# The residual row travels with each expert's rows instead of being read back at the end

## The chip, the cores and the metric

One core of a Trainium2 chip runs the whole program. The metric is the device time of one execution in microseconds; lower is better.

## What is computed

One layer of a hybrid decoder trunk on 512 tokens of width 1024, fp32 throughout: a token-mixing block (attention, convolution, matrix memory), then a hierarchical mixture of experts, then a gated per-layer embedding and a last RMSNorm. The parts that matter here, with `x2` for the residual after token mixing:

```
h2  = rmsnorm(x2) * g_ffn
wts = p_group * softmax(top-2 logits)            # each token goes to 2 of 32 experts
x3  = x2 + sum over its 2 experts of wts * (silu(h2 @ w_gate[e]) * (h2 @ w_up[e])) @ w_down[e]
hp  = rmsnorm(x3) * g_ple
x4  = x3 + sigmoid(hp @ w_ple_gate) * (p @ w_ple_proj)
out = rmsnorm(x4) * g_final
```

## The kernel before

The program is written by hand, engine by engine: the order in which instructions stand in each engine's block is the order in which they run, and semaphores are the only link between engines.

**Experts.** `x2` is stored to `x2_rows` in memory. The 32 experts run one after the other, each on a block of up to 64 tokens. A token's row of 1024 is handled as two halves of 512, so a block fills 128 partitions. For expert n:

- GpSimd (`gather_rows`) gathers the block's rows of `x2` by an indirect DMA into `xr[n % 4]` (`ROWS` = 4 slots).
- TensorE (`turn_block`, L1518) transposes them into one PSUM bank. VectorE (`turned_block`, L2200) scales them into `xT`.
- TensorE (`up`) multiplies by the gate and up weights. ScalarE takes the sigmoid (L1004), VectorE makes the product (`swiglu`, L2207 and L2209), TensorE transposes it (L1538) and ScalarE copies it (L1009).
- TensorE (`down`) multiplies by the down weights. ScalarE (`scale_rows`, L1016) multiplies the result by the routing weight into `yr[n % 4]`, and raises `y_scaled`.
- GpSimd (`scatter_rows`) scatters `yr` into `expert_rows` in memory, which has one row per token for each of its two choices.

TensorE's order in iteration n is `up(n)` (with the transpose of the hidden block of n-1 in its middle), `turn_block(n+1)`, `down(n-1)`. The weights (3 MB per expert) come over SyncE's queue into a ring of 7 slots for gate and up and 9 for down; a load is issued when TensorE has released its slot. Experts with more than 64 tokens would take further blocks in a conditional loop behind; with these inputs that loop runs no block.

**Tail.** After the last `down`, TensorE multiplies `p` by its projection (`ple`, into PA and PB; ScalarE and VectorE copy the halves, L1043 and L2236). `w_ple_gate` is split into a rounded part (`round_pg`, ScalarE, L1024) and a remainder (`pg_remainder`, VectorE, L2230), eight pieces each. When every scatter has landed, SyncE reads back the rows of both choices (`yk[t]`, L671 and L674) and `x2` (`x2_row_back`, L642), in four tiles of 128 tokens. VectorE adds them (L2262, L2263), TensorE transposes the sum (L1405), ScalarE rounds it (`h3_rounding`, L1063), VectorE takes the remainder (L2254), and TensorE runs the eight gate products, each as high x high, low x high and high x low (L1108, `pg_mm`). The factor of the RMSNorm enters as the scale of the sigmoid.

Of the kernel before, what the change touches and what calls it, by code (L numbers as in the profile page):

```python
# [31 lines left out]
ALU = mybir.AluOpType  # L32
ACT = mybir.ActivationFunctionType
AXX = mybir.AxisListType.X

P = 128
D = 1024
SEQ = 512
T = SEQ // P
KD = D // P  # L40
# [10 lines left out]
NEXP = NGROUP * PER_GROUP  # L51
HID = 256
PLE = 256
EPS = 1e-6
# [69 lines left out]
def build(nc, x, consts, chan, g_mix, r_bias, g_final, w_cm, w_tm, w_if, w_gate, w_branch, w_out,  # L124
# [5 lines left out]
    with ExitStack() as ctx:  # L130
# [378 lines left out]
        def _(sp):  # L509
# [130 lines left out]

            def x2_row_back(t):
                sp.dma_start(x_sb[:, t, :], x2_rows[t * P:(t + 1) * P, :]).then_inc(rows_loaded[t], 16)  # L642

            sp.wait_ge(up_done, 28)
# [4 lines left out]
            sp.dma_start(pg_w[1], w_pg[1, :, :]).then_inc(pg_loaded[1], 16)  # L649
            for t in range(2):  # L650
                x2_row_back(t)
            sp.wait_ge(routed, 1)
# [12 lines left out]
            for t in range(T):  # L665
                if t >= 2:
                    x2_row_back(t)
                if t == 0:
                    for cols, loaded in ((slice(0, 512), rows_loaded[0]), (slice(512, D), gmix_then_rows_loaded)):
                        for k in range(2):  # L670
                            sp.dma_start(yk[0][:, k, cols], expert_rows[k * SEQ:k * SEQ + P, cols]).then_inc(loaded, 16)  # L671
                    continue
                for k in range(2):
                    sp.dma_start(yk[t][:, k, :],  # L674
                                 expert_rows[k * SEQ + t * P:k * SEQ + (t + 1) * P, :]).then_inc(rows_loaded[t], 16)
                if t == 1:
                    sp.dma_start(gfin_sb, g_final.partition_broadcast(P)).then_inc(params_loaded, 16)
# [11 lines left out]
        def _(act):  # L689
            roots = [0]  # L690

            def root(dst, total, squared, count):

                roots[0] += 1
                act.wait_ge(squared, count)
                act.activation(dst, total, ACT.Sqrt, scale=1.0 / D, bias=chn[:, EPS_COL:EPS_COL + 1]).then_inc(rooted, 1)

# [312 lines left out]

            def scale_rows(n, b2, slot, scattered):

                act.wait_ge(down_done, n + 1)
                if scattered is not None:
                    act.wait_ge(rows_scattered[slot], scattered)
                act.activation(yr[slot], Y[b2][:, :], ACT.Copy, scale=table_w(0, n)).then_inc(y_scaled, 1)  # L1016

            act.wait_ge(table_ready, 2)
# [8 lines left out]
            for n in range(NEXP + 1):  # L1027
                if n:
                    hidden_copy(n - 1, (n - 1) % 2)
                if n < NEXP:  # L1030
                    gate_sigmoid(n, n % 2)
                if n:
                    m = n - 1
                    scale_rows(m, m % 2, m % ROWS, m // ROWS * 16 if m >= ROWS else None)
                if n == OVER_KNOWN:
                    act.wait_ge(routed, 1)
                    n_over = act.value_load(ctl[0:1, 0:1], min_val=0, max_val=MAX_OVER)
# [13 lines left out]
            with act.If(n_over > 0):  # L1051
                with act.Fori(0, MAX_OVER) as j:
                    with act.If(j < n_over):
                        gate_sigmoid(NEXP + j, 0)
                        hidden_copy(NEXP + j, 0)
                        scale_rows(NEXP + j, 0, 0, SCATTERED + j * 16)

# [8 lines left out]
            for t in range(T):  # L1066
# [5 lines left out]
                act.activation(junk3, x_sb[:, t, :], ACT.Square, accum_out=ss3[:, t:t + 1]).then_inc(x3_squared, 1)  # L1072
            root(rr3, ss3, x3_squared, T)
            act.wait_ge(tail_rstd, 1)
# [572 lines left out]
        def _(dve):  # L1647
# [25 lines left out]

            def rstd(root, total, done=None, offset=EPS):

                rooted_seen[0] += 1
                dve.wait_ge(rooted, rooted_seen[0])
                steps[0] += 1
                dve.tensor_scalar(total, total, 1.0 / D, offset, ALU.mult, ALU.add).then_inc(dve_step, 1)
                chain(dve.reciprocal(root, root))  # L1680
                if root.shape[-1] == 1:
                    chain(dve.scalar_tensor_tensor(total, total, root, root, ALU.mult, ALU.mult))
                else:
                    chain(dve.tensor_tensor(total, total, root, ALU.mult))
                    chain(dve.tensor_tensor(total, total, root, ALU.mult))
                chain(dve.tensor_scalar(total, total, -0.5, 1.5, ALU.mult, ALU.add))
                last = dve.tensor_tensor(root, root, total, ALU.mult)
                if done:
                    last.then_inc(done[0], 1)
                    dve.wait_ge(*done)  # L1690
                else:
                    chain(last)
# [451 lines left out]
            dve.wait_ge(act_step, 7)  # L2144
            chain(dve.tensor_scalar(per[:, 5, 0, :], per[:, 0, 0, :], 1.0, None, ALU.add))
            chain(dve.reciprocal(per[:, 5, 0, :], per[:, 5, 0, :]))
# [58 lines left out]
            def swiglu(n, b2):  # L2205
# [3 lines left out]
                dve.tensor_tensor(hs[b2], GU[b2][:, P:2 * P], sgx[b2], ALU.mult).then_inc(h_swished, 1)  # L2209

            turned_block(0, 0)
            for n in range(NEXP):
                if n + 1 < NEXP:
                    turned_block(n + 1, (n + 1) % 2)
                swiglu(n, n % 2)
                if n == 0:
                    over_slots()
                if n == 1:
                    over_experts()
                if n == 3:  # L2220
                    over_rows()
                if n == OVER_KNOWN:
                    dve.wait_ge(routed, 1)
                    n_over = dve.value_load(ctl[0:1, 0:1], min_val=0, max_val=MAX_OVER)

            def pg_remainder(k):
# [11 lines left out]
            for t in range(3):  # L2238
                ple_second_half(t)
                pg_remainder(2 * t)  # L2240
                pg_remainder(2 * t + 1)
            with dve.If(n_over > 0):
                with dve.Fori(0, MAX_OVER) as j:
                    with dve.If(j < n_over):
                        turned_block(NEXP + j, 0)
                        swiglu(NEXP + j, 0)


# [8 lines left out]
            for t in range(T):  # L2257
                dve.wait_ge(rows_loaded[t], 48)
                for cols in (slice(0, D),) if t else (slice(0, 512), slice(512, D)):
                    if cols.start:  # L2260
                        dve.wait_ge(gmix_then_rows_loaded, 48)
                    chain(dve.tensor_tensor(x_sb[:, t, cols], x_sb[:, t, cols], yk[t][:, 0, cols], ALU.add))  # L2262
                    dve.tensor_tensor(x_sb[:, t, cols], x_sb[:, t, cols], yk[t][:, 1, cols], ALU.add).then_inc(x3_ready, 1)  # L2263
                if t == 0:
                    ple_second_half(3)
                    h3_remainder(0)
                    for k in range(6, KD):
                        pg_remainder(k)
                if t == 1:
                    h3_remainder(1)  # L2270
            rstd(rr3, ss3, (tail_rstd, 1))
            for t in range(T - 1):
                if t == T - 2:
                    h3_remainder(T - 1)
                for half in range(2):
# [4 lines left out]
                    chain(dve.tensor_tensor(ple_rows[t][:, cols], ple_rows[t][:, cols], sg6[:, t % 2, cols], ALU.mult))  # L2280
                dve.tensor_tensor(x_sb[:, t, :], x_sb[:, t, :], ple_rows[t], ALU.add).then_inc(x4_ready, 1)
                if t == 0:
# [7 lines left out]
            for piece, cols in enumerate(LAST_COLUMNS):  # L2290
                dve.wait_ge(pg_sig, 2 * T - 1 + piece)  # L2291
                chain(dve.tensor_tensor(ple_rows[t][:, cols], ple_rows[t][:, cols], sg6[:, 1, cols], ALU.mult))  # L2292
                chain(dve.tensor_tensor(x_sb[:, t, cols], x_sb[:, t, cols], ple_rows[t][:, cols], ALU.add))  # L2293
                dve.tensor_tensor_reduce(out=sg6[:, 0, cols], in0=x_sb[:, t, cols], in1=x_sb[:, t, cols], scale=1.0 / D,  # L2294
# [16 lines left out]
        def _(pool):  # L2311
# [52 lines left out]
            for n in range(NEXP):  # L2364
                slot = n % ROWS
                if n + ROWS < NEXP:
                    pool.wait_ge(rows_turned, n + 1)
                    gather_rows(slot, table[:, 0, n + ROWS:n + ROWS + 1], rows_gathered[slot])
                pool.wait_ge(y_scaled, n + 1)
                scatter_rows(slot, table[:, 1, n:n + 1], rows_scattered[slot])  # L2370
                if n == OVER_KNOWN:
                    pool.wait_ge(routed, 1)
                    n_over = pool.value_load(ctl[0:1, 0:1], min_val=0, max_val=MAX_OVER)
# [93 lines left out]
```

## Time and profile before

| | us |
|---|---|
| median of 3 runs | 933.08 (932.34 to 934.02) |
| the profiled execution | 934.07 |
| its span, first to last instruction | 931.9 |
| mean granted TensorE clock | 0.992 |
| PE busy | 898.1 (96%) |
| DVE busy | 504.0 (54%) |
| ACT busy | 343.2 (37%) |
| POOL busy | 195.8 (21%) |

PE is TensorE, DVE VectorE, ACT ScalarE, POOL GpSimd, SPq SyncE's queue. A busy share over the whole span says little here, since the stages have different limits. The experts run from about 638 to 855 us, the tail from there to the end.

### The profile page before, as it was taken

Reading aid. Unit: us, or ns where it says so; the run is one execution under the profiler, and the core shown is the slowest. Engines: PE = TensorE matmul, PEld = TensorE weight load, DVE = VectorE, ACT = ScalarE, POOL = GpSimd, SP = SyncE. Lnnn points to the kernel's source line nnn. Section 1 sums busy time; section 2 is a strip of 40 time slices with the busy share of each in tenths; the row PEclk is TensorE's granted clock in tenths of the full one; section 3 lists DMA queues with packets and bytes.
Section 4 is the critical chain, followed back from the end, with each engine's and each line's share of the span. In section 5 each row is a group of like instructions: output and inputs, shape, how many; then the busy total and the mean of one; then the engine's idle time right before and its main releaser. Section 6 shows DMA issues by size and latency. Waiting matters only on the chain. (4 is left out here: it accounts for less than half of the span.)

```text
span 931.9 us, 12362 instructions
## 1 busy us (share of the span) xinstructions
PE 898.1 (96%) x4864; PEld 661.8 (71%) x4864; DVE 504.0 (54%) x1043; ACT 343.2 (37%) x571; POOL 195.8 (21%) x169
## 2 busy tenths in 40 slices
PE   6999999999999999999999999999999999888896
PEld 5788788878877887888888888876555555444586
DVE  6378579759767999943333336375112112111766
ACT  5534453535355357622222243121122122112465
POOL 0052263327134433000000000002332332311000
PEclk9999999999999999999999999999999999999899
DMA  7520321122031111541222209959999999999701
GB/s 280 181 91 23 126 78 46 71 88 65 27 114 45 44 60 46 212 167 71 92 102 102 101 9 396 383 198 412 420 417 420 422 416 422 418 421 392 272 23 68
DMA packets 29233, 180.35 MB, mean 194 GB/s; under 512 B 5856, under 2 KB 6368, under 8 KB 18040
## 3 DMA queue, kind: packets, MB, share of 16 engines
q1 hardware_dynamic: 24056, 171.16, 46.8%
q0 software_dynamic: 5120, 8.41, 2.4%
q8 instruction: 39, 0.64, 0.3%
q14 instruction: 18, 0.15, 0.0%
HBM read 175.33 MB, written 12.59 MB: 202 GB/s over the span
## 5 line engine op out<-in xcount | busy, mean ns | idle before, releaser
L1108 PE MATMUL bank<-mT_parts,low_parts 128*128 128x512 f32 (+1 forms) x456 | 178.6, 394 | 0.0
L1108 PE MATMUL bank<-arena,cst 128*64 128x256 f32 (+2 forms) x918 | 133.5, 431 | 7.6 <-DMA arena<-in_w_expert 6.9
L1108 PE MATMUL bank<-mT_parts,x_parts 128*128 128x512 f32 (+1 forms) x328 | 132.7, 405 | 2.8 <-DVE arena L1783 2.3
L1108 PE MATMUL bank<-hT_parts,x_parts 128*128 128x512 f32 (+1 forms) x328 | 129.1, 394 | 0.0
L1718 DVE TENSOR_TENSOR low_parts<-arena,x_parts 128x1024 fp32r<-128x1024 f32 (+1 forms) x44 | 64.6, 1470 | 93.7 <-ACT x_parts L718 93.3
L2200 DVE TENSOR_TENSOR cst<-bank,chn 128x512 f32<-128x512 f32 x32 | 22.1, 692 | 164.8 <-PE bank L1518 164.8
L1108 PEld LDWEIGHTS bank<-arena,cst 128*64 128x64 f32 (+1 forms) x918 | 63.5, 138 | 61.6 <-issue 28.6
L1108 PEld LDWEIGHTS bank<-mT_parts,low_parts 128*128 128x128 f32 (+1 forms) x456 | 84.9, 186 | 21.5 <-DVE low_parts L1718 0.4
L1770 DVE SCALAR_TENSOR_TENSOR arena<-arena,chn 128x512 f32<-128x512 f32 x116 | 99.1, 912 | 0.0
L2351 POOL DMA_INDIRECT mT<-x_rows,table x32 | 33.1, 1034 | 270.5 <-DVE table L2130 257.8
L1108 PE MATMUL bank<-arena 128*128 128x64 f32 (+9 forms) x400 | 79.8, 332 | 0.0
L1108 PEld LDWEIGHTS bank<-mT_parts,x_parts 128*128 128x128 f32 (+1 forms) x328 | 61.0, 186 | 19.6 <-DVE low_parts L1718 3.5
L2336 POOL TENSOR_TENSOR arena<-arena 128x128 f32<-128x128 f32 (+3 forms) x32 | 38.6, 1208 | 172.6 <-ACT arena L814 172.6
L1108 PEld LDWEIGHTS bank<-hT_parts,x_parts 128*128 128x128 f32 (+1 forms) x328 | 61.0, 186 | 15.3 <-issue 1.0
L1108 PEld LDWEIGHTS bank<-arena 128*128 128x128 f32 (+1 forms) x400 | 56.4, 189 | 19.6 <-issue 13.6
L2357 POOL DMA_INDIRECT expert_rows<-mT,table x32 | 32.5, 1016 | 148.9 <-ACT mT L1016 144.3
L814 ACT ACTIVATE arena<-arena,small 128x384 f32<-128x384 f32 (+3 forms) x32 | 32.6, 1020 | 57.0 <-DVE small L1870 56.9
L959 ACT ACTIVATE arena<-bank 128x512 f32<-128x512 f32 x24 | 14.2, 597 | 102.3 <-PE bank L1108 95.2
L1108 PE MATMUL bank<-mT_parts,cm_high_b 128*128 128x512 f32 x128 | 51.2, 409 | 0.3 <-ACT mT_parts L724 0.3
L1108 PE MATMUL bank<-hT_parts,cm_high_b 128*128 128x512 f32 x128 | 49.2, 393 | 0.0
L1016 ACT ACTIVATE mT<-bank,table_weight 128x512 f32<-128x512 f32 x32 | 22.0, 687 | 67.0 <-PE bank L1108 67.0
L1108 PE MATMUL bank<-x_parts,mT_parts 128*128 128x384 f32 x128 | 44.7, 350 | 0.0
(303 smaller groups left out, 1592.7 us busy)
## 6 DMA issues: line engine op xcount, KB each, us to landing
arena<-in_w_expert SPq DMA_DIRECT2D x19, 2048.0 KB, 28.8
arena<-in_w_expert SPq DMA_DIRECT2D x30, 1024.0 KB, 19.9
arena<-in_w_cm SPq DMA_DIRECT2D x32, 512.0 KB, 3.5
arena<-in_w_gate SPq DMA_DIRECT2D x7, 1536.0 KB, 6.7
hT<-in_w_expert SPq DMA_DIRECT2D x4, 2048.0 KB, 24.5
yT<-in_w_expert SPq DMA_DIRECT2D x4, 2048.0 KB, 27.5
arena<-in_w_tm SPq DMA_DIRECT2D x4, 1536.0 KB, 7.1
arena<-in_w_branch SPq DMA_DIRECT2D x8, 768.0 KB, 8.0
```

The costliest lines, as they stand in the source:

```text
L814: act.activation(sc[:, u % 2, 0:n], sc[:, u % 2, 0:n], ACT.Exp, bias=nmx[:, u % 2:u % 2 + 1], accum_out=den[:, u:u + 1]).then_inc(exps_don ...
L959: act.activation(sgm[:, br], (PA, PB, S_16)[br][:, :], ACT.Sigmoid).then_inc(gate_read, 1)
L1016: act.activation(yr[slot], Y[b2][:, :], ACT.Copy, scale=table_w(0, n)).then_inc(y_scaled, 1)
L1108: return pe.matmul(out, lhsT, rhs, start=start, stop=stop)
L1718: dve.tensor_tensor(low, weights, high.bitcast(F32), ALU.subtract).then_inc(done, 1)
L1770: dve.scalar_tensor_tensor(cacc[:, j % 2], ypad[:, j:j + SEQ], weight, cacc[:, j % 2], ALU.mult, ALU.add).then_inc(conv_step, 1)
L2200: dve.tensor_tensor(xT[b2], TR[:, :].rearrange("p (k h s) -> p k h s", k=KD // 2, h=2), chn[:, G_FFN:G_FFN + KD].rearrange("p (h k) -> p k ...
L2336: pool.tensor_tensor(dst[:, 0:n], sc[:, u % 2, 0:n], sc[:, u % 2, n:2 * n], ALU.add).then_inc(pool_step, 1)
L2351: pool.indirect_dma_start(out=xr[slot], out_offset=None, in_=x2_halves, in_offset=bass.IndirectOffsetOnAxis(ap=token_halves, axis=0), boun ...
L2357: pool.indirect_dma_start(out=expert_halves, out_offset=bass.IndirectOffsetOnAxis(ap=row_halves, axis=0), in_=yr[slot], in_offset=None, bo ...
```

## The change

Each expert's result now carries the residual row with it: `weighted_rows` computes `yr = weight * Y + xr` on VectorE, where `xr` is the row gathered for this block. Every token goes to two experts, so the sum of its two rows holds `x2` twice; the routing weights are doubled to match, `x_sb` then holds `2 * x3`, and the tail halves it (the factors in the two RMSNorm roots, 0.5 in the sums that form `x4`). `x2` is no longer read back, and of two additions per tile of the tail one is left. The first two pieces of the diff are SyncE's, the third is ScalarE's, the last is GpSimd's, the others are VectorE's.

```
-            for t in range(2):
-                x2_row_back(t)
...
-                if t >= 2:
-                    x2_row_back(t)
...
-                if n:
-                    m = n - 1
-                    scale_rows(m, m % 2, m % ROWS, m // ROWS * 16 if m >= ROWS else None)
...
-            chain(dve.tensor_scalar(per[:, 5, 0, :], per[:, 0, 0, :], 1.0, None, ALU.add))
+            chain(dve.tensor_scalar(per[:, 5, 0, :], per[:, 0, 0, :], 1.0, 0.5, ALU.add, ALU.mult))
...
+            def weighted_rows(n, b2, slot, scattered):
+                dve.wait_ge(down_done, n + 1)
+                if scattered is not None:
+                    dve.wait_ge(rows_scattered[slot], scattered)
+                dve.scalar_tensor_tensor(yr[slot], Y[b2][:, :], table_w(0, n), xr[slot],
+                                         ALU.mult, ALU.add).then_inc(y_scaled, 1)
...
                 swiglu(n, n % 2)
+                if n:
+                    weighted_rows(n - 1, (n - 1) % 2, (n - 1) % ROWS, (n - 1) // ROWS * 16 if n > ROWS else None)
...
-                    chain(dve.tensor_tensor(x_sb[:, t, cols], x_sb[:, t, cols], yk[t][:, 0, cols], ALU.add))
-                    dve.tensor_tensor(x_sb[:, t, cols], x_sb[:, t, cols], yk[t][:, 1, cols], ALU.add).then_inc(x3_ready, 1)
+                    dve.tensor_tensor(x_sb[:, t, cols], yk[t][:, 0, cols], yk[t][:, 1, cols], ALU.add).then_inc(x3_ready, 1)
...
             for n in range(NEXP):
                 slot = n % ROWS
-                if n + ROWS < NEXP:
-                    pool.wait_ge(rows_turned, n + 1)
-                    gather_rows(slot, table[:, 0, n + ROWS:n + ROWS + 1], rows_gathered[slot])
                 pool.wait_ge(y_scaled, n + 1)
                 scatter_rows(slot, table[:, 1, n:n + 1], rows_scattered[slot])
+                if n + ROWS < NEXP:
+                    gather_rows(slot, table[:, 0, n + ROWS:n + ROWS + 1], rows_gathered[slot])
```

On GpSimd, at the start of the experts, the gathers (mT<-x_rows) and scatters (expert_rows<-mT) stand like this before; `xr` and `yr` both lie in mT:

```order
L2351 DMA mT<-x_rows,table 128x512 [waits x2_spilled,table_ready]
L2351 DMA mT<-x_rows,table 128x512 x3
L2351 DMA mT<-x_rows,table 128x512 [waits rows_turned]
L2357 DMA expert_rows<-mT,table 2048x512 [waits y_scaled]
L2351 DMA mT<-x_rows,table 128x512 [waits rows_turned]
L2357 DMA expert_rows<-mT,table 2048x512 [waits y_scaled]
```

and like this in the changed kernel:

```order
L2348 DMA mT<-x_rows,table 128x512 [waits x2_spilled,table_ready]
L2348 DMA mT<-x_rows,table 128x512 x3
L2354 DMA expert_rows<-mT,table 2048x512 [waits y_scaled]
L2348 DMA mT<-x_rows,table 128x512
L2354 DMA expert_rows<-mT,table 2048x512 [waits y_scaled]
```

Five gathers stood ahead of scatter 0 and four do now. The gather for expert n+4 stood right behind scatter n-1 and needed only the transpose of expert n; it now stands behind scatter n, and so behind `y_scaled` of expert n.

On VectorE, between the last expert and the products of the tail, before:

```order
L2230 SCALAR_TENSOR_TENSOR pg_low_57<-arena,chn,pg_high_59 128x1024 [waits rounded] x2
...
L2262 TENSOR_TENSOR x_sb<-x_sb,arena 128x512 [waits rows_loaded0]
L2263 TENSOR_TENSOR x_sb<-x_sb,arena 128x512 [waits dve_step]
L2262 TENSOR_TENSOR x_sb<-x_sb,arena 128x512 [waits gmix_then_rows_loaded]
L2263 TENSOR_TENSOR x_sb<-x_sb,arena 128x512 [waits dve_step]
L2236 COPY arena<-bank 128x512 [waits ple_mm]
L2254 TENSOR_TENSOR hT_parts<-bank,mT_parts 128x4x128 [waits h_rounded] x2
L2230 SCALAR_TENSOR_TENSOR pg_low_57<-arena,chn,pg_high_59 128x1024 [waits rounded] x2
```

and in the changed kernel:

```order
L2259 TENSOR_TENSOR x_sb<-arena 128x512 [waits rows_loaded0]
L2259 TENSOR_TENSOR x_sb<-arena 128x512 [waits gmix_then_rows_loaded]
L2225 SCALAR_TENSOR_TENSOR pg_low_57<-arena,chn,pg_high_59 128x1024 [waits rounded]
L2231 COPY arena<-bank 128x512 [waits ple_mm]
L2251 TENSOR_TENSOR hT_parts<-bank,mT_parts 128x4x128 [waits h_rounded] x2
L2225 SCALAR_TENSOR_TENSOR pg_low_57<-arena,chn,pg_high_59 128x1024 [waits rounded] x3
```

Two remainder pieces stood ahead of the first addition and now stand behind it; the first tile takes two additions where it took four.

## Rows read from the trace of the kernel before

**Rows 1.** Page, part 2: DMA in 40 slices, mean busy share in tenths

```profile
DMA  7520321122031111541222209959999999999701
```

**Rows 2.** TensorE's timeline: start us, us, engine, line, what, count, wait and releaser

```profile
668.01 0.66 PE L1518 MATMUL bank<-cst,mT 128*128 128x128 f32 x4
...
775.43 0.66 PE L1518 MATMUL bank<-cst,mT 128*128 128x128 f32 x4
...
777.79 1.90 PE L1108 MATMUL bank<-yT,cst 128*64 128x256 f32 x16
```

**Rows 3.** Timeline of all engines, 699 to 713 us

```profile
702.17 0.69 ACT L1016 ACTIVATE mT<-bank,table_weight 128x512 f32<-128x512 f32 x1 [2.09 <-PE bank L1108]
703.66 1.02 POOL L2357 DMA_INDIRECT expert_rows<-mT,table  x1 [3.97 <-ACT mT L1016]
...
704.99 1.03 POOL L2351 DMA_INDIRECT mT<-x_rows,table  x1 [0.30 <-issue]
...
712.24 0.66 PE L1518 MATMUL bank<-cst,mT 128*128 128x128 f32 x4
```

**Rows 4.** The gathers (L2351) from 664 to 860 us: landing time

```profile
L2351 POOL DMA_INDIRECT mT<-x_rows,table x25: 1025/1029/1044, 667.1 to 823.0; - x25
...
DMA to landing us min/median/max: 7.9/9.2/10.7
```

**Rows 5.** The gathers from 638 to 664 us: landing time of three

```profile
DMA to landing us min/median/max: 6.9/7.6/9.2
```

**Rows 6.** GpSimd's timeline: the gather behind scatter 1

```profile
659.82 1.03 POOL L2351 DMA_INDIRECT mT<-x_rows,table  x1 [0.30 <-issue]
```

**Rows 7.** TensorE's timeline, late experts and the first products of the tail

```profile
822.22 3.63 PE L1108 MATMUL bank<-arena,cst 128*64 128x256 f32 x16 [2.12 <-DMA arena<-in_w_expert]
...
846.22 1.95 PE L1108 MATMUL bank<-arena,cst 128*64 128x256 f32 x16 [1.38 <-DMA arena<-in_w_expert]
...
855.31 7.13 PE L1108 MATMUL bank<-hT 128*128 128x512 f32 x16 [0.35 <-DMA hT<-in_pT]
863.24 7.13 PE L1108 MATMUL bank<-hT 128*128 128x512 f32 x16 [0.80 <-ACT yT L1043]
```

**Rows 8.** DMA issues, 630 to 860 us: KB each, median us to landing

```profile
arena<-in_w_expert SPq DMA_DIRECT2D x16, 2048.0 KB, 32.0
```

**Rows 9.** VectorE's scalar_tensor_tensor of 128x512: ns min/median/max

```profile
L1770 DVE SCALAR_TENSOR_TENSOR arena<-arena,chn x116: 735/747/1787, 68.2 to 344.9; 128x512 f32<-128x512 f32 x116
```

**Rows 10.** Timeline of the start of the tail

```profile
860.52 2.19 ACT L1024 ACTIVATE pg_high<-arena,chn 128x1024 fp32r<-128x1024 f32 x2 [2.51 <-DMA arena<-in_w_pg]
...
864.16 1.75 SPq L671 DMA_DIRECT2D arena<-expert_rows  x4
864.19 0.10 POOL L2391 MEMSET small<- 128x1 f32 x1 [6.74 <-DMA expert_rows<-mT,table]
...
869.19 2.17 ACT L1024 ACTIVATE pg_high<-arena,chn 128x1024 fp32r<-128x1024 f32 x2
...
870.08 0.68 DVE L2262 TENSOR_TENSOR x_sb<-x_sb,arena 128x512 f32<-128x512 f32 x1
...
873.57 0.60 ACT L1063 ACTIVATE mT_parts<-bank 128x512 fp32r<-128x512 f32 x1 [0.67 <-PE bank L1405]
...
874.22 3.78 PE L1108 MATMUL bank<-pg_high,mT_parts 128*128 128x512 f32 x8 [0.69 <-ACT mT_parts L1063]
874.81 2.47 DVE L2230 SCALAR_TENSOR_TENSOR pg_low<-arena,chn,pg_high 128x1024 fp32r<-128x1024 f32 x2
...
880.79 2.03 PE L1108 MATMUL bank<-pg_low,mT_parts 128*128 128x512 f32 x8
```

**Rows 11.** Windows: busy us of PE, PEld, DVE, ACT, POOL, PEclk, DMA share, GB/s

```profile
664.00:804.00 140.00, 139.23 (x992) 71.41 (x988) 25.96 (x66) 29.99 (x67) 45.05 (x44) 1.00 1.01 420
```

**Rows 12.** Windows of 1 us in the tail, the same columns

```profile
863.00:864.00 1.00, 0.76 (x2) 0.49 (x3) 1.00 (x1) 1.00 (x2) 0.00 (x0) 1.00 0.28 115
...
875.00:876.00 1.00, 1.00 (x4) 0.81 (x3) 1.00 (x2) 0.20 (x2) 0.00 (x0) 0.50 1.04 426
```

More of the change, by code:

```diff
@@ L639, in _ @@
             down_weights(NEXP - 1)
-            def x2_row_back(t):
-                sp.dma_start(x_sb[:, t, :], x2_rows[t * P:(t + 1) * P, :]).then_inc(rows_loaded[t], 16)
             sp.wait_ge(up_done, 28)
@@ L690, in _, with root @@
             roots = [0]
-            def root(dst, total, squared, count):
+            def root(dst, total, squared, count, scale=1.0 / D):
                 roots[0] += 1
                 act.wait_ge(squared, count)
-                act.activation(dst, total, ACT.Sqrt, scale=1.0 / D, bias=chn[:, EPS_COL:EPS_COL + 1]).then_inc(rooted, 1)
+                act.activation(dst, total, ACT.Sqrt, scale=scale, bias=chn[:, EPS_COL:EPS_COL + 1]).then_inc(rooted, 1)
             act.wait_ge(cell_set, 1)
@@ L1009, in hidden_copy @@
                 act.activation(hx[b2], HT[:, 0:P].rearrange("p (j s) -> p j s", j=2), ACT.Copy).then_inc(hx_ready, 1)
[L1011 to L1016, printed above, removed]
             act.wait_ge(table_ready, 2)
@@ L1055, in _ @@
                         hidden_copy(NEXP + j, 0)
-                        scale_rows(NEXP + j, 0, 0, SCATTERED + j * 16)
             def h3_rounding(t):
@@ L1072, in _ @@
                 act.activation(junk3, x_sb[:, t, :], ACT.Square, accum_out=ss3[:, t:t + 1]).then_inc(x3_squared, 1)
-            root(rr3, ss3, x3_squared, T)
+            root(rr3, ss3, x3_squared, T, 0.25 / D)
             act.wait_ge(tail_rstd, 1)
@@ L1672, in _, with rstd @@
             rooted_seen = [0]
-            def rstd(root, total, done=None, offset=EPS):
+            def rstd(root, total, done=None, offset=EPS, factor=1.0):
                 rooted_seen[0] += 1
@@ L1678, in rstd @@
                 steps[0] += 1
-                dve.tensor_scalar(total, total, 1.0 / D, offset, ALU.mult, ALU.add).then_inc(dve_step, 1)
+                dve.tensor_scalar(total, total, factor * factor / D, offset, ALU.mult, ALU.add).then_inc(dve_step, 1)
                 chain(dve.reciprocal(root, root))
@@ L1686, in rstd @@
                 chain(dve.tensor_scalar(total, total, -0.5, 1.5, ALU.mult, ALU.add))
-                last = dve.tensor_tensor(root, root, total, ALU.mult)
+                last = (dve.tensor_tensor(root, root, total, ALU.mult) if factor == 1.0 else
+                        dve.scalar_tensor_tensor(root, root, factor, total, ALU.mult, ALU.mult))
                 if done:
@@ L2224, in _ @@
                     n_over = dve.value_load(ctl[0:1, 0:1], min_val=0, max_val=MAX_OVER)
+            weighted_rows(NEXP - 1, (NEXP - 1) % 2, (NEXP - 1) % ROWS, (NEXP - 1) // ROWS * 16)
             def pg_remainder(k):
@@ L2239, in _ @@
                 ple_second_half(t)
-                pg_remainder(2 * t)
-                pg_remainder(2 * t + 1)
+                if t < 2:
+                    pg_remainder(2 * t)
+                    pg_remainder(2 * t + 1)
             with dve.If(n_over > 0):
@@ L2246, in _ @@
                         swiglu(NEXP + j, 0)
+                        weighted_rows(NEXP + j, 0, 0, SCATTERED + j * 16)
             def h3_remainder(t):
@@ L2257, in _ @@
             for t in range(T):
-                dve.wait_ge(rows_loaded[t], 48)
+                dve.wait_ge(rows_loaded[t], 32)
                 for cols in (slice(0, D),) if t else (slice(0, 512), slice(512, D)):
@@ L2261, in _ @@
                         dve.wait_ge(gmix_then_rows_loaded, 48)
-                    chain(dve.tensor_tensor(x_sb[:, t, cols], x_sb[:, t, cols], yk[t][:, 0, cols], ALU.add))
-                    dve.tensor_tensor(x_sb[:, t, cols], x_sb[:, t, cols], yk[t][:, 1, cols], ALU.add).then_inc(x3_ready, 1)
+                    dve.tensor_tensor(x_sb[:, t, cols], yk[t][:, 0, cols], yk[t][:, 1, cols], ALU.add).then_inc(x3_ready, 1)
                 if t == 0:
+                    pg_remainder(4)
                     ple_second_half(3)
                     h3_remainder(0)
-                    for k in range(6, KD):
+                    for k in range(5, KD):
                         pg_remainder(k)
@@ L2270, in _ @@
                     h3_remainder(1)
-            rstd(rr3, ss3, (tail_rstd, 1))
+            rstd(rr3, ss3, (tail_rstd, 1), factor=0.5)
             for t in range(T - 1):
@@ L2280, in _ @@
                     chain(dve.tensor_tensor(ple_rows[t][:, cols], ple_rows[t][:, cols], sg6[:, t % 2, cols], ALU.mult))
-                dve.tensor_tensor(x_sb[:, t, :], x_sb[:, t, :], ple_rows[t], ALU.add).then_inc(x4_ready, 1)
+                dve.scalar_tensor_tensor(x_sb[:, t, :], x_sb[:, t, :], 0.5, ple_rows[t], ALU.mult, ALU.add).then_inc(x4_ready, 1)
                 if t == 0:
@@ L2292, in _ @@
                 chain(dve.tensor_tensor(ple_rows[t][:, cols], ple_rows[t][:, cols], sg6[:, 1, cols], ALU.mult))
-                chain(dve.tensor_tensor(x_sb[:, t, cols], x_sb[:, t, cols], ple_rows[t][:, cols], ALU.add))
+                chain(dve.scalar_tensor_tensor(x_sb[:, t, cols], x_sb[:, t, cols], 0.5, ple_rows[t][:, cols], ALU.mult, ALU.add))
                 dve.tensor_tensor_reduce(out=sg6[:, 0, cols], in0=x_sb[:, t, cols], in1=x_sb[:, t, cols], scale=1.0 / D,
```

## The prediction

> **What bounds the kernel now.** I read first the busy shares in 40 slices, and there the DMA row [rows 1]: it stands at 9 from about 640 to 855 us, the stage of the experts, so this stage seems to end when the weights have come. Then TensorE's own timeline in it [rows 2]: the transposes of expert 5 stand at 668.01 and those of expert 22 at 775.43, so TensorE takes 107.42 / 17 = 6.32 us per expert, and in the windows it is busy for 139.23 of the 140 us up to 804, at full clock [rows 11]. So up to there TensorE bounds and the weights are ahead; the ring hides that they come more slowly. Then it turns, and TensorE waits for weights again and again [rows 7]; the gate and up products of expert 31 start at 846.22 behind such a wait. At TensorE's own pace the transposes of expert 31 would have stood at 668.01 + 26 x 6.32 = 832.3, and its products 2.36 later (777.79 - 775.43 [rows 2]), at 834.7. So 846.22 - 834.7 = 11.5 us is the reserve that TensorE has over the weights: a slower TensorE in this stage costs nothing until it has lost 11.5 us.
>
> Behind the experts the tail is a chain: the projection of p from 855.31 on [rows 7], then additions, transposes and roundings to the first gate product at 874.22 [rows 10]. From 874.22 to the span's end it is 57.7 us.
>
> **The gathers, the step that decides.** The timeline of one expert shows the loop [rows 3]. Two experts before the transposes at 712.24, so at 699.60, stand the transposes of an expert I call m. ScalarE scales the result of m-2 at 702.17, GpSimd scatters it at 703.66, and right behind, at 704.99, it issues a gather: today that of m+3, in the changed kernel that of m+2. Nothing else in these times moves, only which expert the gather is for. Today it has 18.96 - 5.39 = 13.6 us until TensorE needs it (three experts behind 699.60). Then it has 712.24 - 704.99 = 7.25 us.
>
> How long does a gather take? The landing time of the 25 gathers between 664 and 860 us is 7.9 at least, 9.2 in the median and 10.7 at most [rows 4]; even the fastest misses 7.25. Today that is covered by the 13.6. So the wait for y_scaled puts the landing of a gather on TensorE's path, where it is not today. Queued behind TensorE's wait are down(n-1), thus the next y_scaled, and thus the gather after next. That closes a loop over two experts: 5.39 us from transposes to gather (704.99 - 699.60), and 9.2 until it lands and the transposes two experts on can start, 14.6 us instead of 12.64. Odd and even experts each have their own such loop, so no expert escapes, and the pace is 7.3 us per expert instead of 6.32.
>
> Sum: the gather of expert 5 is the one behind scatter 1, at 659.82 [rows 6]; it is among the three of 6.9 to 9.2 [rows 5], and with 9.2 it lands at 669.0, 1.0 behind 668.01. From there 26 experts at 7.30 give 189.8: the transposes of expert 31 at 858.8, its products at 861.2. Today 846.22. The stage loses 15.0 us: 26.5 us of waiting, less the reserve of 11.5.
>
> Does the stream of weights bear it? It is the cover for all this, and it stays ahead: a load of 2 MB lands 32 us after its issue [rows 8], so there are about four experts in the queue, and a slot that comes free at most 15 us later leaves a backlog. TensorE then waits for gathers, not for weights, and at the end the weights of the tail have been there for long.
>
> Bounds of this term. Each us of landing time is half a us per expert, 13 us over 26. With 7.9 throughout the loop is 13.3 us, expert 31 starts at 669.0 + 26 x 6.65 + 2.36 = 844.3, inside today's 846.22: nothing lost. With 10.7 it is 16.1 us, 880.7, or 34 us lost. Neither end can be the rule, since medians count here, and I take 9.2; with 0.5 us more or less on the mean it is 6.5 us either way.
>
> **The weighting.** 32 activations of 0.69 us [rows 3] leave ScalarE, 32 scalar_tensor_tensor of 128x512 come to VectorE. The trace has this operation from SBUF only, 0.735 at least, 0.747 in the median, 1.787 at most [rows 9]. In the loop above it replaces the 0.69, so it costs between 0.05 and 1.1 us per two experts, 0.6 to 14 us over 13 loops. The long ones belong to a stage where GpSimd computes; here it waits just then for this very result, so I take 0.05 and 1 us in all. VectorE has 26 of 140 us of work in the stage [rows 11], and the operation stands behind the product of its own iteration and ahead of a wait for transposes that come later than its operand; it delays nothing else. What ScalarE saves, it saves while waiting.
>
> **The residual not read back.** Two of the four reads (1 MB) went behind the second half of the gate weights; the DMA engines have run down to a share of 0.28 at 863 [rows 12], ahead of the reads of the rows at 864.16 [rows 10]. Worth nothing. The other two stand between the reads of tiles 1 to 3, whose additions are far from TensorE's path. Also nothing.
>
> **The tail.** Today, at the first tile, three things meet: VectorE is in its remainders until 870.08, ScalarE in its last pieces of rounding until 869.19 + 2.17 = 871.36, and then come additions of 0.68 in pairs [rows 10]. With two additions gone and two remainders behind them, ScalarE is what is late next: its two roundings of the first tile, 0.60 each, could end at 872.6, so 1.6 us are won at 874.22. With the shift of the experts another count holds. The projection starts 846.22 to (855.31 - 0.35) = 8.7 us behind the products of expert 31, at 861.2 + 8.7 + 1 = 870.9. Its eight halves take 14.26 / 8 = 1.78 us each [rows 7]; the seventh ends 12.5 later, then a copy (0.60), the last two pieces (2.17) and two roundings (1.2), with some 0.3 for hand-overs: 16.8, so the first gate product starts at 887.7. Scatter, read of the rows and the addition run beside the projection. Today there are 18.9 us from projection to product, so 2.1 us come back here.
>
> A second gain is the clock. Today TensorE idles for parts of 870.4 to 874.2, and the granted clock falls to 0.50 (1.2 GHz) [rows 12]: the first two groups of eight products take 3.78 and 3.15 where 2.03 is the time at full clock [rows 10], from 874.22 to 880.79 in place of 4.1 us. With the transposes of the first tile right behind the projection and some 1.3 us idle, I let the clock stay up: 2.5 us. The three remainders moved behind (2.47 for two [rows 10]) end about 4 us after the first product, the third group begins then and asks for them one by one: no wait. From the first product to the end remain 57.7 - 2.5 = 55.2 us. The halving adds nothing that could be seen on VectorE: the same instruction count, 128x256 to 128x1024.
>
> Total: span 887.7 + 55.2 = 942.9, against 931.9, so 11 us more. The profiled execution took 934.07 with its 931.9; that gives 945.1. The median of the runs is 1.0 below the profiled one: 944.1. I say 945.
>
> **A rule that speaks against it.** The Trainium skill, DMA: Bandwidth & Descriptors, in Anatomy of one DMA, gives a software-generated DMA about 2.0 us fixed plus its bytes over 436e3 per us. By that estimate a gather of 256 KB would land in 2.6 us, far inside 7.25, and the new order would cost nothing; the time would be that of the first rival. The trace disagrees: with the weights streaming beside them the gathers take 9.2 us, and the measurement decides.
>
> **The rivals.**
> 1. The gathers stay hidden: once TensorE waits, their landing shrinks to 7.9 or less, the loop is 13.3 us, and the weights set the end as today. For it: three gathers landed in 6.9 to 9.2 near 640 to 660 [rows 5]. Against: the pair scatter and gather goes out as now, 1.3 us apart, beside a full stream. It decides at 8.1 us of mean landing: (846.22 - 2.36 - 669.0) x 2 / 26 = 13.45, less 5.39. Then only the tail moves: 1.6 us earlier and up to 2.5 of clock, 930 to 932.5. Chance 0.09, of which 0.01 lies within 0.2% of 933 (about what a measurement of this kernel can tell from no change), and 0.04 that it comes to rest there from above.
> 2. The clock falls in the new waits. A wait of 2.12 us for weights was followed by 16 products in 3.63 us where 1.95 is usual, while one of 1.38 went without [rows 7]. The waits here are about 1 us per expert, or 2 at every second. If a third of 26 fall so, 9 x 1.7 = 15 us come on top where they lie in the loop, half of it if they lie beside: 953 to 960. Chance 0.13.
> 3. The weighting takes up to 1.1 us longer in VectorE: 959. Chance 0.03.
> My case, 0.71, alone is 938 to 952. The range 936 to 957 reaches into rival 2. Faster 0.08, same 0.05, slower 0.87.
>
> **What would show it.** In the changed kernel, transposes in the experts waiting for DMA mT<-x_rows, about 1 us per expert, 25 us in all; transposes 7.3 us apart; no wait of the products for weights any more in the late experts; the projection at 871 instead of 855; ScalarE's last pieces straight ahead of its roundings; full clock behind the first gate product. Wrong would be: waits for weights as before, or landings of the gathers below 8 us.

## The result and the profile after

| | before | changed |
|---|---|---|
| median of 5 runs, us | 932.34 (930.96 to 934.02) | 947.79 (945.38 to 949.22) |
| the profiled execution | 934.07 | 947.79 |
| its span | 931.9 | 945.9 |
| TensorE's projection of p starts | 855.31 | 875.05 |
| first gate product | 874.22 | 891.07 |
| from there to the span's end | 57.7 | 54.8 |

The changed kernel is slower: the ratio is 1.0158, 95% interval 1.0143 to 1.0173. The forecast was 945 in a range of 936 to 957.

The page's part 2, the rows for DMA and the clock; the DMA row answers to [rows 1]:

```profile
PEclk9999999999999999999999999999999899999998
DMA  7520321222031111732222039779999999985501
```

The nines of the DMA row no longer reach the end of the experts' stage: the row shows 5 from about 851 us on, ahead of the end of the last expert at 875 us. Who waited for whom on TensorE, from 638 to 880 us (us in total, times, longest):

```profile
PE bank L1500 <- DMA mT<-x_rows,table: 24.1, 17, 2.9
PE bank L1090 <- DVE cst L2183: 0.9, 1, 0.9
PE bank L1500 <- issue: 0.7, 2, 0.5
PE bank L1090 <- issue: 0.4, 1, 0.4
```

L1500 are the transposes of gathered rows (L1518 before). Of the waits for weights, which stood at 6.9 and 1.8 us in the same view of the kernel before, none is left. One turn of the loop, from the timeline around 700 us, to be laid beside [rows 3]:

```profile
697.52 0.66 PE L1500 MATMUL bank<-cst,mT 128*128 128x128 f32 x4 [1.08 <-DMA mT<-x_rows,table]
...
700.09 0.75 DVE L2199 SCALAR_TENSOR_TENSOR mT<-bank,table_weight,mT 128x512 f32<-128x512 f32 x1 [0.66 <-PE bank L1090]
701.64 1.02 POOL L2354 DMA_INDIRECT expert_rows<-mT,table  x1 [5.11 <-DVE mT L2199]
...
702.97 1.03 POOL L2348 DMA_INDIRECT mT<-x_rows,table  x1 [0.31 <-issue]
...
705.25 0.66 PE L1500 MATMUL bank<-cst,mT 128*128 128x128 f32 x4 [1.34 <-DMA mT<-x_rows,table]
...
713.28 0.66 PE L1500 MATMUL bank<-cst,mT 128*128 128x128 f32 x4 [1.65 <-DMA mT<-x_rows,table]
```

From transposes to the gather that the transposes two experts on will need it is 5.45 us (702.97 - 697.52; 5.39 before), and those transposes start 10.31 us behind that gather's issue (713.28 - 702.97). Laying each of the gathers for experts 8 to 26 beside its transposes, 14 of them end in a wait for this DMA, and there the time from issue to transposes is 9.6 us in the mean. This trace has no landing times for the gathers. A second trace of the same kernel (the one of experiment 4) has them, here for the 18 gathers issued from 690 to 836 us:

```profile
DMA to landing us min/median/max: 7.6/9.5/10.7
```

### The profile page after: what moved, and what is told of

It reads as the page before. It is cut to its first block and busy times, and to the rows that moved or that the text cites. A ratio compares the mean times of both kernels' runs of the same rounds, so it can differ in the third digit from the quotient of the medians.

```text
span 945.9 us, 12353 instructions
## 1 busy us (share of the span) xinstructions
PE 898.9 (95%) x4864; PEld 661.2 (70%) x4864; DVE 522.9 (55%) x1070; ACT 321.2 (34%) x539; POOL 195.8 (21%) x169
## 5 line engine op out<-in xcount | busy, mean ns | idle before, releaser
L1090 PE MATMUL bank<-arena,cst 128*64 128x256 f32 (+2 forms) x918 | 136.4, 438 | 0.4 <-issue 0.4
L1090 PEld LDWEIGHTS bank<-arena 128*128 128x128 f32 (+1 forms) x400 | 56.4, 189 | 19.6 <-issue 13.6
L1002 ACT ACTIVATE cst<-bank 128x128 f32<-128x128 f32 x32 | 8.9, 278 | 158.9 <-PE bank L1520 131.3
L1500 PE MATMUL bank<-cst,mT 128*128 128x128 f32 x128 | 21.5, 291 | 24.8 <-DMA mT<-x_rows,table 24.1
```

What stands on the lines that cost most here:

```text
L1002: act.activation(hx[b2], HT[:, 0:P].rearrange("p (j s) -> p j s", j=2), ACT.Copy).then_inc(hx_ready, 1)
L1090: return pe.matmul(out, lhsT, rhs, start=start, stop=stop)
L1500: last = pe.transpose(TR[:, k * P:(k + 1) * P], xr[slot][:, k * P:(k + 1) * P], ident)
```

## Experiments

Each kernel ran beside the kernel before on the same chip; ratios are to it.

**1. Only the order on GpSimd.** The kernel before with

```
-                if n + ROWS < NEXP:
-                    pool.wait_ge(rows_turned, n + 1)
-                    gather_rows(slot, table[:, 0, n + ROWS:n + ROWS + 1], rows_gathered[slot])
                 pool.wait_ge(y_scaled, n + 1)
                 scatter_rows(slot, table[:, 1, n:n + 1], rows_scattered[slot])
+                if n + ROWS < NEXP:
+                    gather_rows(slot, table[:, 0, n + ROWS:n + ROWS + 1], rows_gathered[slot])
```

> The kernel before, with one edit: each gather stands behind the scatter of the expert four ahead of it, as in the changed kernel; the weighting stays on ScalarE, the residual is read back, the tail is unchanged. My theory (the landing of the gathers on TensorE's path): TensorE waits some 24 us in all for gathers, the projection starts at about 874 us instead of 855, and the tail is one or two us longer than in the changed kernel, since its additions are four again: 947 to 950 us. Rival (the loss comes from the weighting on VectorE or from something in the tail): the order costs nothing, 932 to 934.

Measured: 952.70 (947.5 to 953.83), ratio 1.0207 (1.0177 to 1.0238). TensorE's waits, 638 to 880 us:

```profile
PE bank L1518 <- DMA mT<-x_rows,table: 26.3, 18, 3.9
```

The whole loss is there without any other part of the change, and more of it than with them. The median is 2.7 us above the top of the expected range. Against the changed kernel's trace there are two more us of waiting (26.3 and 24.1), and 17.7 us from the projection (877.06) to the first product (894.80) where the changed kernel takes 16.0; that second part was expected. TensorE's work ran slowly behind four of the waits, at a cost of 6.6 us, about what it cost the changed kernel behind three (6.5, experiment 4). The rival is out.

**2. The gather ahead of the scatter.** The changed kernel with

```
                 pool.wait_ge(y_scaled, n + 1)
-                scatter_rows(slot, table[:, 1, n:n + 1], rows_scattered[slot])
                 if n + ROWS < NEXP:
                     gather_rows(slot, table[:, 0, n + ROWS:n + ROWS + 1], rows_gathered[slot])
+                scatter_rows(slot, table[:, 1, n:n + 1], rows_scattered[slot])
```

> The changed kernel with the pair on GpSimd turned round: once y_scaled of expert n has come, first the gather of expert n+4, then the scatter of expert n. The gather goes out 1.3 us earlier and is no longer behind the scatter's packets in its queue. My theory: the loop over two experts is 4.1 us plus the landing; with a landing still at 9.2 it is 13.3 (6.65 us per expert, TensorE waits some 8 us in all, which the reserve of 11.5 absorbs), with a landing at 8.0, as the scatter has today, 12.1, below 12.64, and no wait is left. So the loss goes either way: 929 to 934 us. Rival (the order has nothing to do with the loss, or any gather behind y_scaled is too late): 943 to 948.

Measured: 930.42 (928.6 to 931.56), ratio 0.9975 (0.9965 to 0.9986). Two transfers changed places, and 17 us are gone. The waits of TensorE from 664 to 855 us, then the gathers and the scatters of this kernel (664 to 860 us) with their landing times:

```profile
PE bank L1090 <- DMA arena<-in_w_expert: 3.7, 3, 1.7
PE bank L1500 <- DMA mT<-x_rows,table: 2.2, 3, 1.1
PE bank L1090 <- DMA hT<-in_w_expert: 2.1, 1, 2.1
PE bank L1090 <- DMA yT<-in_w_expert: 1.6, 1, 1.6
```

```profile
L2348 POOL DMA_INDIRECT mT<-x_rows,table x26: 1020/1025/1042, 665.8 to 830.9; - x26
...
DMA to landing us min/median/max: 7.5/8.1/9.7
```

```profile
L2354 POOL DMA_INDIRECT expert_rows<-mT,table x30: 977/1016/1021, 667.1 to 857.3; - x30
...
DMA to landing us min/median/max: 7.7/9.2/10.3
```

The gather goes out 4.1 us behind the transposes, which leaves 12.64 - 4.1 = 8.5 us, and lands in 8.1: just in time, with three waits left. The 9.2 us of [rows 4] now belong to the scatter. So about 1 us of the landing time goes with the place in the pair, and not with the direction of the transfer.

**3. A fifth slot.** The changed kernel with a fifth buffer for gathered rows, and the gather of expert n+4 ahead of the wait for y_scaled of n, as before:

```
+GATHERED = 5
...
+        xr.append(nc.alloc_sbuf_tensor_at("xr5", [P, 512], F32, offset=offset_of["wr_sb"])[:, :])
...
+                if n + ROWS < NEXP:
+                    ahead = (n + ROWS) % GATHERED
+                    if n == 0:
+                        pool.wait_ge(xT_ready, 1)
+                    gather_rows(ahead, table[:, 0, n + ROWS:n + ROWS + 1], rows_gathered[ahead])
                 pool.wait_ge(y_scaled, n + 1)
                 scatter_rows(slot, table[:, 1, n:n + 1], rows_scattered[slot])
```

> The changed kernel with a fifth slot for gathered rows (in memory that the router has left) and GpSimd's order as before: the gather of expert n+4 stands ahead of scatter n and needs only y_scaled of n-1. The rest of the change stays (weighting on VectorE, no read-back, shorter tail). My theory: no wait for gathers, TensorE at 6.32 us per expert, weights late again from about 805 us on, projection at 855, and the tail by 1.6 us (ScalarE late next) to 4 us (clock up as well) shorter than before: 928.5 to 931.5 us. Rival (the weighting on VectorE costs the path in the loop): 936 or more. Rival (the gain of the tail does not exist where the experts end at 855): 932 to 933.

Measured: 930.01 (928.74 to 932.08), ratio 0.9979 (0.9966 to 0.9991); a second time 930.26, ratio 0.9980 (0.9969 to 0.9992). The transposes of two experts, two apart, around 700 us with the weighting between them, then the landing of the gathers (664 to 860 us):

```profile
699.49 0.65 PE L1502 MATMUL bank<-cst,mT 128*128 128x128 f32 x4
...
702.06 0.75 DVE L2201 SCALAR_TENSOR_TENSOR mT<-bank,table_weight,mT 128x512 f32<-128x512 f32 x1 [0.67 <-PE bank L1092]
...
712.12 0.66 PE L1502 MATMUL bank<-cst,mT 128*128 128x128 f32 x4
```

```profile
L2351 POOL DMA_INDIRECT mT<-x_rows,table x20: 1026/1026/1042, 667.0 to 822.4; - x20
L2351 POOL DMA_INDIRECT xr<-x_rows,table x5: 1026/1026/1029, 679.7 to 806.0; - x5
...
DMA to landing us min/median/max: 7.8/9.2/11.0
```

Its scatters, first in the pair, land in 8.1 us in the median. The gathers land no faster than before, yet TensorE is back at 6.32 us per expert (12.63 for two) with the weighting on VectorE in its place. So neither the weighting nor the landing time alone is the cause; it is the wait for y_scaled ahead of a landing that long. This kernel and that of experiment 2 are faster than both the changed kernel and the kernel before, than the latter by about 2 us.

**4. Fillers against the clock.** In the changed kernel three waits are followed by slow work. The longest, and the window behind it (busy PE, PEld, DVE, ACT, POOL, clock, DMA share, GB/s):

```profile
736.71 1.12 PE L1500 MATMUL bank<-cst,mT 128*128 128x128 f32 x4 [2.92 <-DMA mT<-x_rows,table]
737.75 6.25 PE L1090 MATMUL bank<-arena,cst 128*64 128x512 f32 x24
```

```profile
738.00:741.00 3.00, 3.00 (x8) 0.75 (x8) 1.04 (x3) 0.00 (x0) 0.00 (x0) 0.50 1.06 436
```

The 24 products take 3.66 at full clock; the granted clock is 0.50, so 1.2 GHz. The four slow groups behind the three waits took 6.0 us more than their full-clock times, the slow transposes 0.5. The edit puts three products that nobody uses, fillers, ahead of the wait for each gather from iteration 5 to 26:

```
                     slot = (n + 1) % ROWS
+                    if 5 <= n <= 26:
+                        pe.wait_ge(xT_ready, n + 1)
+                        for q in range(3):
+                            mm(TR[:, 0:P], ident, ident)
```

> The changed kernel, with three products of 128x128 into the transposes' bank ahead of TensorE's wait for each gather, for iterations 5 to 26 (about 0.8 us each, results overwritten). In the changed kernel's trace the granted clock falls in three of the waits, of 2.92, 1.92 and 1.91 us, and the work behind takes 3.1, 1.7 and 1.9 us longer. Theory: the idle time in the waits brings the clock down; with 0.8 us of it filled the falls become rarer, and since the pace of 7.3 us per expert leaves room for 0.8 more (7.1), the time falls by up to 6 us: 940 to 946. Rival: the falls do not depend on these 0.8 us, or the fillers delay the experts that had no wait (nine of 26, up to 7 us): 947 to 954.

> The changed kernel once more, unchanged, as the measure for the one beside it on the same chip: 945 to 949 us.

> The changed kernel with three filler products ahead of each wait for a gather in iterations 5 to 26, once more, beside the changed kernel on the same chip. If the falls of the clock cost the changed kernel the 6.6 us that its trace shows behind three waits, and the fillers take them away without a price of their own: 4 to 6 us less than the kernel beside it. If the fillers only put busy time where idle time was and cost at the experts without a wait what they save in clock: within 2 us of it.

Measured: 946.24 (945.84 to 947.85), ratio 1.0148 (1.0129 to 1.0168), between the two ranges of the first expectation; then side by side 948.04 (946.17 to 948.54), ratio 1.0163 (1.0149 to 1.0177), against the changed kernel's 949.40 (946.3 to 951.28), ratio 1.0180 (1.0160 to 1.0200), just above the 945 to 949 expected for it. The first time the fillers' trace has one fall (1.7 us), 11.2 us of waiting and 22 fillers of 0.78 us, 17 us:

```profile
PE bank L1500 <- DMA mT<-x_rows,table: 11.2, 15, 2.1
```

11.2 + 17 + 1.7 = 30 us against 24.1 + 6.5 = 31 without them, and the projection starts at 875.06 against 875.05. The second pair of traces says the same: 10.0 us of waiting, 17 of fillers and 3.4 of slow work behind two waits make 30, and the changed kernel beside it has 23.0 us of waiting and 7.9 of slow work behind four waits, 31. The fillers took most of the slow work away and gave it back at the experts that had no wait, which now took about 7.03 instead of 6.32. 1.4 us lie between the medians, and the intervals overlap: of the last expectation's two cases the second holds, within 2 us. The slow work was 6.5 us in one trace of the changed kernel and 7.9 in the other; what it cost in the executions without a trace stays open.

**5. The tail apart.** Three kernels, run beside experiment 3's:

> The kernel with five slots once more, unchanged, as the measure for the three beside it on the same chip. 929.5 to 930.5 us by every theory.

*The read-back alone.* Five slots, with the four reads of x2 and their place in SyncE's order restored:

```
+                sp.dma_start(x_sb[:, t, :], x2_rows[t * P:(t + 1) * P, :]).then_inc(rows_loaded[t], 16)
...
-                dve.wait_ge(rows_loaded[t], 32)
+                dve.wait_ge(rows_loaded[t], 48)
```

> The kernel with five slots, with the four reads of the residual put back where the kernel before has them; what they bring is not used (the addition overwrites it), only waited for. Prices the removed read-back alone. My theory: nothing, since the DMA engines run down to a share of 0.28 ahead of the rows; at most 0.5 us over the kernel beside it. Rival: 1 MB of it lies behind the last gate weights beside the last scatters, and 0.5 MB ahead of the rows of tile 2, and delays the last landing by up to 2.4 us (1 MB at the 420 GB/s of the stage): 1 to 2.5 us more.

Measured: 930.54 (929.31 to 933.64), ratio 0.9987 (0.9975 to 0.9999), beside 930.26: 0.3 us. The read-back was hidden, as far as these runs can tell.

*The remainders in the old order.* Five slots, with

```
-                if t < 2:
-                    pg_remainder(2 * t)
-                    pg_remainder(2 * t + 1)
+                pg_remainder(2 * t)
+                pg_remainder(2 * t + 1)
```

and pieces 6 and 7 alone behind the additions.

> The kernel with five slots, with the remainder pieces 4 and 5 back ahead of the first additions on VectorE. Theory: the additions then start at about 869.6 instead of 867.9 and end at 871.0 instead of 870.6, the first gate product comes 0.4 us later, since ScalarE and the landing of the second half bound it already: within 0.5 us of the kernel beside it. Rival: this order is what wins in the tail, by 1.5 us and by keeping the clock up (2.5 us more): 931.5 to 934.

Measured: 930.31 (928.43 to 931.66), ratio 0.9975 (0.9964 to 0.9986): no difference.

*The remainders' order alone*, on the kernel before (the opposite edit).

> The kernel before, with only the remainder pieces 4 to 7 moved behind the first additions on VectorE as in the changed kernel; residual read back, four additions for the first tile. Theory: the additions start when the rows have landed, at about 868.5 instead of 870.1, the first gate product comes at about 873.0 instead of 874.2, and TensorE's pause is short enough that the clock stays up (2.5 us): 928.5 to 931. Rival: the rows land too late for it, or the clock falls as before: 931.5 to 933.

Measured: 932.93 (930.57 to 936.94), ratio 1.0011 (0.9997 to 1.0026). A miss: no gain. Its profiled execution took 930.92, near its fastest, and there TensorE's first gate products ran at full clock; in the profiled execution of the kernel before this one in the list, five slots with the old order (931.66, its slowest), they did not. The first row is of this kernel, the second of the old-order kernel's:

```profile
873.62 2.13 PE L1108 MATMUL bank<-pg_high,mT_parts 128*128 128x512 f32 x8 [0.69 <-ACT mT_parts L1063]
```

```profile
873.39 3.68 PE L1092 MATMUL bank<-pg_high,mT_parts 128*128 128x512 f32 x8 [0.69 <-ACT mT_parts L1047]
```

The last wait ahead of both is the same 0.69 us. With the waits ahead of the two groups of transposes before it, the idle time is 2.1 us here and 1.5 in the old-order kernel, and it is the shorter one that had the clock down. So one profiled execution does not say whether this pause brings the clock down in most runs, and the span of one execution must not be taken for the gain of a kernel: the first profile of experiment 3 is 5.0 us shorter than that of before, its median 2.1.

## Why the prediction was right

**The gathers.** As forecast: transposes wait for the gather DMA, 24.1 us where the list of signs has 25, at odd and even experts alike, and no wait for weights is left. Experiments 1 to 3 show it from three sides: the order alone brings the loss, and either an earlier place in the pair or one more slot takes it away. The reserve was real too: experiment 2's kernel waits for weights again at the end.

**Its size.** Transposes of expert 31 at 864.41, forecast 858.8. Until expert 8 the forecast was near (690.06, forecast 690.9). From there to expert 27 the pace was not 7.30 but (838.31 - 690.06) / 19 = 7.80: 9.5 us more than forecast. Of them 6.5 are the slow work behind three waits and 2.0 are waiting: the waits for gathers in this stretch sum to 20.6 us, and 19 x (7.30 - 6.32) = 18.6 was forecast. About 1 us is left over. That the waiting is longer fits a landing of 9.5 in the median in the second trace, where I had put 9.2. From expert 27 to 31 it was 26.1 us instead of 29.2: there the queue of weights runs out, and the last four transposes start 7.2 to 8.0 us behind the issue of their gathers, one of them after a wait of 0.76. The two windows show it, same columns as above:

```profile
690.00:836.00 146.00, 125.12 (x838) 62.62 (x838) 36.66 (x76) 11.61 (x36) 37.51 (x37) 0.95 1.01 420
836.00:860.00 24.00, 23.24 (x166) 11.87 (x164) 6.96 (x15) 2.58 (x8) 7.54 (x8) 1.00 0.74 291
```

The second trace of this kernel has the landing of the last four gathers, issued from 836.6 to 857.0 us:

```profile
DMA to landing us min/median/max: 2.8/6.6/7.5
```

I had the stream "stay ahead", which it did, but not that it ends early and frees the last gathers. In all, the products of expert 31 start at 864.41 + 2.36 = 866.8 and TensorE has lost 866.8 - 834.7 = 32.1 us, where the sum has 26.5: the term for the waits was close (24.1 measured), and the clock was missing beside it.

**The clock.** I put it in a rival of nine falls and 15 us and left it out of the sum. It was three falls and 6.5 us in the profiled execution and four and 7.9 in the second: right mechanism, about half of the time, and it belonged into the sum. The length of a wait does not sort them: 1.91 and 1.92 us were followed by slow work, 2.19 and 2.33 were not.

**The weighting.** The operation on a PSUM and an SBUF operand:

```profile
L2199 DVE SCALAR_TENSOR_TENSOR mT<-bank,table_weight,mT x32: 749/750/752, 650.3 to 875.2; 128x512 f32<-128x512 f32 x32
```

0.750 each, 0.06 more than ScalarE's 0.69; I had taken 0.05. No long ones, so rival 3 is out.

**The tail.** Projection 8.3 us behind the products of expert 31 instead of 9.7, of which 1 us was put there for the weighting and did not appear. From it to the first product 16.0, forecast 16.8, with ScalarE's last pieces at 887.87 straight ahead of the roundings, as forecast:

```profile
887.87 2.18 ACT L1010 ACTIVATE pg_high<-arena,chn 128x1024 fp32r<-128x1024 f32 x2
888.89 1.04 PE L1387 MATMUL bank<-cst,x_sb 128*128 128x128 f32 x8
...
889.95 1.07 ACT L1045 ACTIVATE mT_parts<-bank 128x512 fp32r<-128x512 f32 x2
...
891.07 2.13 PE L1090 MATMUL bank<-pg_high,mT_parts 128*128 128x512 f32 x8 [1.14 <-ACT mT_parts L1045]
893.04 2.02 PE L1090 MATMUL bank<-pg_high,hT_parts 128*128 128x512 f32 x8
```

The first two groups take full-clock times where they were 3.78 and 3.15 [rows 10]. From there to the end 54.8, forecast 55.2. The errors add to +5.6 (stage), -1.4, -0.8 and -0.4, so 3 us in the span, the 945.9 against 942.9. That the forecast came so close is in part luck: the stage alone was 9.5 us out up to expert 27, and an end of the stream that the prediction did not have gave 3.1 of them back.

**The read-back and the order of the remainders.** The read-back was forecast at nothing, and 0.3 us were measured. The order of the remainders had no term of its own, only one of 1.6 us together with the additions, and by itself it measured nothing (both in experiment 5). What makes the repaired kernels (experiments 2 and 3) 2 us faster than the kernel before is then the additions or what they do to the clock at the first product; the last run of experiment 5 did not separate the two, but the runs on record say more. Where the first groups have full clock, the time from the first product to the span's end is 54.8 to 55.1 us in every trace, with four additions in the first tile as with two; with the clock down it is 57.7 before and 56.4 in the old-order kernel. From the projection to the first product the five-slot kernels take 17.3 to 17.9 us, the kernel before 18.9, and the one with only the remainders moved 18.4. And among the executions with a mean granted clock of 0.998 or more, experiment 3's kernel has a median of 929.9 (6 executions) beside 931.5 (8) of the kernel before: 1.6 of the 2.1 us are there at equal clock. That they come from the additions fits these times, but no run has the additions alone, and it stays not shown.

**Rival 1** fell: gathers waited for did not shrink to 8.1 us, except where the stream had ended. Its threshold of 8.1 us was not tested: the gathers of experiment 2 land in 8.1, but they also go out 1.3 us earlier and have 8.5 to go. The time is that of the rival, 930.4. The Trainium skill (DMA: Bandwidth & Descriptors, Anatomy of one DMA) gives 2.6 us by its fit, an estimate for 256 KB. Beside the stream of weights the trace disagrees: in every trace that has their landing, the gathers issued between 690 and 836 us take 7.5 us at least. Once the stream has ended it agrees: in the second trace the last gather, issued at 856.98 us where the DMA share is 0.28 (857 to 860 us), lands in 2.8 us, and so does the last one of experiment 1.

## What to carry to other kernels

When a buffer is read a second time later in its life, look at who was waiting to refill it: the cost of the new reader can be the refill's landing time, not the reader's own 0.75 us. Subtract the landing time that the loaded queue really shows from the time between the new release and the next need; where the rest is negative, add a slot or issue the refill ahead of everything else in its queue, and only then look at what the change saves. A landing time read at one end of the stage need not hold at the other: here it was 9.5 us beside the full queue and 2.8 behind it.

## What the runs showed of the hardware that was not expected

- Of an indirect gather and an indirect scatter of 256 KB at most, issued 1.3 us apart beside a full stream, the first lands in 8.1 us and the second in 9.2 (medians), whichever of them it is: the gather was first in experiment 2, the scatter in experiment 3, and the gather second in [rows 4].
- The same gather lands in 2.8 us once the weights have come (the last one of the changed kernel's second trace and of experiment 1), against 9.5 in the median beside them.
- Waits of TensorE for gathers of 1.91 to 2.92 us were followed by a clock of 0.50 in three cases, and in two of 2.19 and 2.33 us not. In the other traces with such waits (experiments 1 and 4) eleven of 1.78 to 3.93 us were followed by slow work, and one of 2.59 us was not. None of those up to 1.74 us was.
- The spread of one kernel's executions (930.6 to 936.9 for the remainders' order alone) is wider than what its edit could bring, and a profiled execution can lie at either end of it.
